# Two transformer blocks in fp32 on one core: earlier weight splits, norm scales left in PSUM, and a reworked program end

## The reference

```python
def hybrid_layer(x, ...):                       # first block
    h = rmsnorm(x, g_pre_mix);  proj = h @ w_in
    y_a = s5_mixer(...); y_b = short_conv_mixer(...); y_c = forgetting_attention(...)
    merged = sum(sigmoid(gate_i) * (y_i @ w_branch_i) for the 3 branches)
    x = x + rmsnorm(merged @ w_out, g_post_mix)
    ff = square(relu(rmsnorm(x, g_pre_mlp) @ w_ff1)) @ w_ff2
    return x + rmsnorm(ff, g_post_mlp)

def second_block(x, ...):
    h = rms_norm(x, norm_mix_pre);  z = h @ w_in
    # chunk_band_attention, hgrn2, spatial_gating, rg_lru_branch: 4 branches of width 256
    merged = sum(sigmoid(gate_n) * (out_n @ w_branch_n) for the 4 branches)
    x = x + rms_norm(merged @ w_out, norm_mix_post)
    gt, up = split(rms_norm(x, norm_ffn_pre) @ w1)
    return x + rms_norm((silu(gt) * up) @ w2, norm_ffn_post)
```

## Time and profile before

| | us |
|---|---|
| three runs | 3702.2, 3705.89, 3710.4 |
| median | 3705.89 |
| the profiled execution | 3706.02 |
| span in its profile | 3704.3 |
| mean PEclk | 0.977 |

### The profile page before, as it was taken

How to read it: one execution, slowest core, us unless ns; L and a number is a source line. 1 busy time by engine, 2 the same in 40 slices (tenths; PEclk the granted TensorE clock), 3 DMA queues, 4 the chain that set the end, 5 groups by cost and what they waited for, 6 DMA issues and landing times. The chain is left out here.

```text
span 3704.3 us, 40483 instructions
## 1 busy us (share of the span) xinstructions
PE 3508.4 (95%) x16092; PEld 2820.4 (76%) x16092; DVE 1446.7 (39%) x1591; ACT 873.6 (24%) x1068; POOL 895.3 (24%) x421
## 2 busy tenths in 40 slices
PE   6989999998998999999989998999999899999996
PEld 5767788887876888888867877777777588888885
DVE  7723565655315222212153446463552521121123
ACT  3112222223313111111232222212342411111111
POOL 2101111111341222222312114231245222222223
PEclk9979999999999999999999999999999999999998
DMA  2534343324421111111224213113253211111122
GB/s 109 148 70 158 109 147 126 100 88 167 146 91 73 47 45 51 45 51 45 91 97 124 92 66 120 63 69 125 99 199 136 74 45 51 45 51 45 45 79 102
DMA packets 105056, 336.81 MB, mean 91 GB/s; under 512 B 15232, under 2 KB 25344, under 8 KB 104848
## 3 DMA queue, kind: packets, MB, share of 16 engines
q1 hardware_dynamic: 101344, 329.78, 26.4%
q10 hardware_dynamic: 3584, 5.25, 0.5%
HBM read 250.37 MB, written 87.62 MB: 91 GB/s over the span
## 5 line engine op out<-in xcount | busy, mean ns | idle before, releaser
L270 POOL TENSOR_TENSOR w_lo<-w_raw,w_hi 128x1024 fp32r<-128x1024 f32 x276 | 686.6, 2488 | 2492.2 <-ACT w_hi L268 2492.2
L307 PE MATMUL pair<-act_hi,w_hi 128*128 128x512 f32 x2992 | 971.4, 406 | 18.9 <-issue 7.0
L307 PE MATMUL pair<-act_lo,w_hi 128*128 128x512 f32 x2992 | 946.5, 397 | 0.0
L307 PE MATMUL pair<-act_hi,w_lo 128*128 128x512 f32 x2992 | 945.1, 397 | 0.0
L307 PEld LDWEIGHTS pair<-act_lo,w_hi 128*128 128x128 f32 x2992 | 566.4, 189 | 138.6
L307 PEld LDWEIGHTS pair<-act_hi,w_lo 128*128 128x128 f32 x2992 | 565.4, 189 | 138.7
L307 PEld LDWEIGHTS pair<-act_hi,w_hi 128*128 128x128 f32 x2992 | 547.7, 190 | 142.7 <-issue 23.5
L268 ACT CAST w_hi<-w_raw 128x1024 fp32r<-128x1024 f32 x276 | 288.9, 1047 | 785.9 <-PE pair L307 709.6
L571 DVE TENSOR_TENSOR p<-pair,rs 128x1024 f32<-128x1024 f32 x100 | 122.1, 1221 | 435.6 <-PE pair L307 428.5
L1791 DVE TENSOR_TENSOR f2v<-pair,rs 128x1024 f32<-128x1024 f32 x42 | 51.4, 1224 | 346.6 <-PE pair L307 346.6
L307 PE MATMUL pair<-f1hh,w_hi 128*128 128x512 f32 x480 | 147.8, 389 | 0.0
(11 more groups left out here) (464 smaller groups left out, 4086.6 us busy)
## 6 DMA issues: line engine op xcount, KB each, us to landing
w_raw<-in_stream SPq DMA_DIRECT2D x278, 512.0 KB, 3.5
proj<-p SPq DMA_DIRECT2D x101, 512.0 KB, 2.6
m2g<-proj SPq DMA_DIRECT2D x32, 512.0 KB, 4.7
foxx<-proj SPq DMA_DIRECT2D x32, 256.0 KB, 5.5
m1g<-proj SPq DMA_DIRECT2D x16, 512.0 KB, 3.3
x<-f1y SPq DMA_DIRECT2D x16, 512.0 KB, 2.6
act_lo<-x SPq DMA_DIRECT2D x16, 512.0 KB, 7.8
m1l<-mixed SPq DMA_DIRECT2D x12, 512.0 KB, 9.2
```

The lines of the kernel that those rows point to most:

```text
L270: nc.gpsimd.tensor_tensor(wlo[:, slot, :], raw[:, slot, :], whi[:, slot, :].bitcast(F32), ALU.subtract).then_inc(s_split, 1)
L307: last = nc.tensor.matmul(out_pair[:, h * HALF:(h + 1) * HALF], wt, a[:, h * HALF:(h + 1) * HALF], start=k == 0 and n_pass == 0, stop=k == ...
```

## The change

Five edits.

1. `split_unit` of unit b+2 is issued at the last tile of unit b, which is the product that frees the slot, and ahead of that block's `evict`; the split of b+1 at the first tile of b goes. In `TwoBlocks` both blocks issue the split at their end, POOL's subtraction in four pieces of 256 columns.
2. The row of scales isn't copied to SBUF: DVE's multiplications in `bridge` read it in PSUM. `lag` for half 1 is 8 instead of 4, so that all tiles of the head's second block for half 1 come after the step loop.
3. `mix_out`'s tail evictions go from DVE (L1741) to ACT.
4. In the last bridge the gain is multiplied in with the scale (one `scalar_tensor_tensor` from PSUM), the residual is added in a second instruction, for k = 1, 3 and 5 on POOL, and every half of 256 KB is stored by itself. The last square goes into the sums by a matmul of its own instead of through POOL.
5. The stream's last two empty units aren't fetched, and the final waits are for two fewer.

```diff
     def split_unit(b, slot, fills, pieces=1):
...
+        n = KT * P // pieces
+        for at in range(0, KT * P, n):
+            last = nc.gpsimd.tensor_tensor(wlo[:, slot, at:at + n], raw[:, slot, at:at + n],
+                                           whi[:, slot, at:at + n].bitcast(F32), ALU.subtract)
+        last.then_inc(s_split, 1)
...
                 if w == 0:
-
-                    split_unit(b + 1, 1 - slot, i * (per_turn // 2) + ((base + n // 8 + 1) // 2 + 1))
                     fetch_unit(b + 3, 1 - slot)
...
+                if w == 7 or (not packed and k == tiles - 1):
+                    split_unit(b + 2, slot, i * (per_turn // 2) + ((base + n // 8 + 2) // 2 + 1))
                 yield
             evict(i, o, out_pair, ready, reads.mark)
...
             if not self.begun:
                 self.begun = True
-                split_unit(b + 1, 1 - slot, (b + 1) // 2 + 1)
-                fetch_unit(b + 3, 1 - slot)
+                if b == 0:
+                    split_unit(1, 1, 1)
+                if not self.final:
+                    fetch_unit(b + 3, 1 - slot)
...
-                    if o == 0:
-                        split_unit(b + 2, slot, b // 2 + 2)
+                    if not self.final:
+                        split_unit(b + 2, slot, b // 2 + 2, 4)
+                    if o == 0 and not self.final:
                         fetch_unit(b + 4, slot)
...
-        y_scale = [A.mark(A.after(spread).copy(r[:, halves[0]], bank[0][:])), None]
+        y_scale = [spread, None]
...
-        lag = (2, 4)
+        lag = (2, KT)
...
-            V.mark(V.after(y_scale[h]).tensor_tensor(yk, yk, r[:, half], ALU.mult))
+            if not next_gain:
+                scaled = V.mark(V.after(y_scale[h], x_ready[k]).scalar_tensor_tensor(yk, yk, col(gain, k), bank[h][:],
+                                                                                     ALU.mult, ALU.mult))
+                if k in (1, 3, 5):
+                    added[h, k] = G.mark(G.after(scaled, x_ready[k]).tensor_tensor(yk, yk, x(k)[:, half], ALU.add))
+                else:
+                    added[h, k] = V.mark(V.then().tensor_tensor(yk, yk, x(k)[:, half], ALU.add))
+                SP.wait_ge(*added[h, k])
+                stores[k % 2].mark(SP.dma_start(out_dram[k][:, half], yk))
+                return
+            V.mark(V.after(y_scale[h]).tensor_tensor(yk, yk, bank[h][:], ALU.mult))
...
-            if k == 3:
+            if k == 3 and next_gain:
                 sums = half_sums(bank[1][:], squares[:, halves[1]], True, True, summed)
+            if k == 2 and not next_gain:
+                half_sums(bank[1][:], squares[:, halves[1]], True, False, summed)
+                sums = half_sums(bank[1][:], last_square[0], False, True, last_square[1])
             if k == 4:
                 root = half_root(1, bank[1][:], 1.0 / D, sums)
             if k == 6:
-                spread = half_spread(1, bank[1][:], root)
-            if k == 7:
-                y_scale[1] = A.mark(A.after(spread).copy(r[:, halves[1]], bank[1][:]))
+                y_scale[1] = half_spread(1, bank[1][:], root)
...
-            square_sum(dst, sq[:, half], squares[:, half], read(V.after(ready).tensor_copy(dst, psum)))
+            square_sum(dst, sq[:, half], squares[:, half], read(A.after(ready).copy(dst, psum)))
...
+                if not next_gain and o and half.start:
+                    a = read(V.after(ready).tensor_tensor(dst, dst, psum, ALU.add))
+                    last_square.extend([sq[:, half], A.mark(A.after(a, G.last()).activation(sq[:, half], dst, ACT.Square))])
+                    return
...
-    for s, n in ((0, (used["units"] + 4) // 2), (1, (used["units"] + 3) // 2)):
+    for s, n in ((0, (used["units"] + 2) // 2), (1, (used["units"] + 1) // 2)):
         SP.wait_ge(s_raw[s], 16 * n)
```

More of the change, by code:

```diff
@@ L263, in _build, with split_unit @@
     used = {"units": 0, "blocks": 0}
-    def split_unit(b, slot, fills):
+    def split_unit(b, slot, fills, pieces=1):
         nc.scalar.wait_ge(s_raw[slot], 16 * fills)
@@ L269, in split_unit @@
         nc.gpsimd.wait_ge(s_whi, b + 3)
-        nc.gpsimd.tensor_tensor(wlo[:, slot, :], raw[:, slot, :], whi[:, slot, :].bitcast(F32),
-                                ALU.subtract).then_inc(s_split, 1)
+        n = KT * P // pieces
[3 more added lines that the diff above has]
+        last.then_inc(s_split, 1)
     def fetch_unit(b, slot):
@@ L391, in _build, with __init__ @@
     class TwoBlocks:
-        def __init__(self, tiles, rhs):
-            self.tiles, self.rhs = tiles, rhs
+        def __init__(self, tiles, rhs, final=False):
+            self.tiles, self.rhs, self.final = tiles, rhs, final
             self.base, self.begun = used["units"], False
@@ L463, in half_spread, with bridge @@
         return PE.mark(last)
-    def bridge(tail, tail_evict, y, squares, x, x_ready, r, sq, gain, out_dram, next_gain, head=None, head_evict=None):
+    def bridge(tail, tail_evict, y, squares, x, x_ready, sq, gain, out_dram, next_gain, head=None, head_evict=None,
+               last_square=None):
         halves = [slice(h * HALF, (h + 1) * HALF) for h in range(2)]
@@ L1714, in __init__ @@
             self.x = sb(at, name + "v", [P, 2, L])
-        def scale_row(self):
-            return self.x[:, 1, :]
         def square_row(self, h, n):
@@ L1740, in tail_evict @@
             dst = y[:, 6 + o, half]
-            square_sum(dst, sq[:, half], squares[:, half], read(V.after(ready).tensor_copy(dst, psum)))
+            square_sum(dst, sq[:, half], squares[:, half], read(A.after(ready).copy(dst, psum)))
         stage(3, 2, 2, KT, rhs, evict, per={A: 2, G: 2})
         bridge(TwoBlocks(KT, act_rhs), tail_evict, y, squares, lambda k: late.hl[:, k, :].bitcast(F32), x_ready,
-               late.scale_row(), late.square_row, gain, out_dram, next_gain, TwoBlocks(KT, act_rhs), head_evict)
+               late.square_row, gain, out_dram, next_gain, TwoBlocks(KT, act_rhs), head_evict)
     def first_hidden(late, gated):
@@ L1834, in mlp @@
                     e.wait_ge(s_mm, used["units"] + 2)
-        tail = TwoBlocks(tiles, hidden_rhs)
+        last_square = []
+        tail = TwoBlocks(tiles, hidden_rhs, final=not next_gain)
         bridge(tail, tail_evict, acc, squares, lambda k: act_lo[:, k, :].bitcast(F32), x_ready,
-               late.scale_row(), late.square_row, gain, out_dram, next_gain,
-               TwoBlocks(KT, act_rhs) if next_gain else None, head_evict)
+               late.square_row, gain, out_dram, next_gain,
+               TwoBlocks(KT, act_rhs) if next_gain else None, head_evict, last_square)
     def first_rows(dst, row, buf):
@@ L1991, in _stream @@
         parts += [w1[g:g + m], np.pad(w2[:, g:g + m], ((0, 0), (0, 8 - m), (0, 0), (0, 0)))]
-    tiles = np.concatenate([p.reshape(-1, P, P) for p in parts] + [np.zeros((3 * 8, P, P), np.float32)])
+    tiles = np.concatenate([p.reshape(-1, P, P) for p in parts] + [np.zeros((8, P, P), np.float32)])
     return _units(tiles)
```

## The result

The changed kernel takes 3719.87 us (median of five, 3718.85 to 3730.13), the one before 3705.51 (3702.2 to 3710.4). The ratio over all runs is 1.0048, 95% interval 1.0031 to 1.0065 (of the two medians alone 1.0039): slower. The forecast was 3712 with a range of 3688 to 3721, 47% for no change and 29% for slower. The time is inside the range, but the kernel became 14.4 us longer, where 6.1 were forecast. The profiled execution has a span of 3717.5 us, 13.2 more than before.

What follows compares the result with a forecast made beforehand. PE, busy 95% of the span, was taken to bound the kernel. Merge 2 +23.7, bridges -6.4, the end -9.5, the chain -1.7 and woven parts 0 gave +6.1 on 3706.02: 3712 us, range 3688 to 3721.

Steps and rivals of the forecast that it cites:

- Merge 2: Merge 2: POOL's moved subtraction stops DVE's two-SBUF-input addition seven times, +15.2 us; with slow clock +23.7.
- The clock: Merge 2: PE idle times of 2.96 us followed by half clock in five of seven cases, +8.5 us.
- Bridges: Bridges A, B, C: `w_lo` waits go, the scale copy is saved, lag 8 costs some; -6.4 us in all.
- The lag's price: Bridges A to C: with `lag` 8, four half tiles no longer fill PE's `act_lo` waits, +4.2 us.
- the sign that I named for it: Bridges: more of PE's idle time released by `act_lo` for half 1 would show the forecast right.
- The end: Last bridge to program end: no `w_lo` wait or slow stretch behind it, shorter additions and stores, -9.5 us.
- The chain: First block's step-size chain: the split now runs before L582, which POOL's subtraction had slowed, -1.7 us.
- the term for the woven parts: Attention, scans, merge 1, feed-forward: later ACT work and DVE meeting POOL are covered by PE's products; 0, +-4 us.
- slower elsewhere too: Scans and attention: subtractions at unit ends also stop DVE where PE waits for it, 2.2 us each; 3722, chance 20%.

Runs made afterwards that it cites:

- e1: The changed kernel with merge 2's last gated product written to PSUM instead of SBUF: 3696.05 us, 0.9969 of the kernel before.
- e13: e5b with the early split in merge 2 as well, whole subtractions: 3712.60 us, 1.0012 of the kernel before.
- e2: The changed kernel with the splits of all products behind the eviction again, the bridges' still early: 3702.84 us, 0.9985 of the kernel before.
- e8b: e5b with the lag for half 1 back at 4 instead of 8: 3683.95 us, 0.9940 of the kernel before.
- e14: e5b with early splits in the woven products too, late in both merges: 3694.38 us, 0.9961 of the kernel before.
- e5b: The changed kernel with early splits only in looped stages and bridges, late in woven products and merges: 3689.10 us, 0.9950 of the kernel before.
- e15: e14 with one split, at unit 39's end in the second block, put behind its eviction: 3693.68 us, 0.9957 of the kernel before.
- e3: The changed kernel with POOL's subtraction cut from 1024 columns to 32: 3635.43 us, 0.9809 of the kernel before.
- e4: The kernel before with POOL's subtraction cut from 1024 columns to 32: 3628.86 us, 0.9792 of the kernel before.
- e10: The changed kernel with POOL's subtraction in quarter pieces in every unit: 3682.15 us, 0.9938 of the kernel before.
- e9: The same program as e5b, measured a second time: 3687.33 us, 0.9949 of the kernel before.
- e7b: The kernel before with POOL's subtraction in four pieces of 256 columns in every unit: 3681.27 us, 0.9928 of the kernel before.
- e12: e5b with lag 4 and POOL's subtraction in eight pieces of 128 columns in every unit: 3654.61 us, 0.9865 of the kernel before.

## Why the prediction was right and wrong

- **Merge 2, right in mechanism and size.** Chain, lead (0.12 us measured, 0.08 forecast), length of the addition (3.36 against 3.40) and PE's idle time (2.92 against 2.96) came as worked out, seven times; e1 and e13 show cause and price, 24 us each.
- **The clock, right in sum by luck.** 24.9 - 14.9 = 10.0 us against 8.5, five of seven followed by slow stretches, as chosen. But the reason given, that 2.96 lies on the low side of 2.40 and 2.82, isn't one: the same 2.92 did both, and two of the five slow stretches were twice as long as reckoned.
- **Bridges, right in sign, too small** (-9.7 against -6.4). `w_lo` went as forecast. e2 keeps the quarter pieces, the reads from PSUM and the lag, and its bridges are 0.7 us longer than before, where the forecast had -0.6 for these; so the early split ahead of the bridges gave some 10.4 us, where I had put 5.8 for the waits alone. The lag's price was right in size (3.8 to 8.3 by e8b, against 4.2). The idle time released by `act_lo` hardly moved as a whole (31.3 to 30.5 us), so the sign that I named for it didn't show.
- **The end, right**: -10.7 against -9.5; by e2, 6.4 of it is the early split (5.1 forecast) and 4.3 the other edits (4.4 forecast). From the last product's end to the spread 8.7 us passed instead of the forecast 9.1.
- **The chain, right in sign**: -3.9 against -1.7; two stops went (L582, L587), and slow clock with them. With whole subtractions it comes only with early woven splits (-3.8 in e14, -0.1 in e5b).
- **The step that failed** is the term for the woven parts: "PE has a unit's 11 us of products before it needs most of them. I take 0, with +-4." The woven stretches came to about +12.5 us; the misses of the other terms took 5.5 of that back (merge 2 +1.2, bridges -3.3, the end -1.2, the chain -2.2), so that the sum was only 7.1 us off. Two premises were wrong. The first is a reading: "most CASTs of weights already start at the end of the product that frees their slot". It was 110 of 276, and the change made it 249. The second is the price, one CAST or 1.05 us later. That held for the copy (+0.96), but a CAST also makes what stands behind it wait for PE: the squares stood behind 4.96 us of waiting and then the CAST. The cover isn't there where a stage's own chain runs through the three engines and PE waits for that chain, not for a product's eviction. Moving a split ahead of `evict` also moves it ahead of whatever the stage has put into ACT's and POOL's queues before the next tile.
- **What the runs put in its place**: a CAST ahead of other work in ACT's queue (2.15 us at the squares, shown by e15, and 0.96 at a copy), POOL's queue held ahead of a scan's additions (1.4 us; e3, e4 and e10 speak for it, no run moved that one split), and slow stretches behind them. The rival "slower elsewhere too" named the place, and 3722 was near; but it named DVE's stops as the cause. At the three places looked at PE waited for what stood in the queues of ACT and POOL behind a split, and in the feed-forwards 107 us of stops cost nothing. I gave it 20%.
- **Only part of the +12.5 us hangs on the woven splits.** The second block's +8.6 does: with these splits early that stretch grew by 8.6, 5.1 and 2.8 us (the change, e14, e1) with +4.9 to +5.6 of idle time each, with them late by -0.7 to +0.9 (e2, e5b, e9, e13) with none. The +3.2 of the other stretches doesn't: they are 3.2 and 3.1 us longer in e5b and e9 too, where the woven splits are late, and 2.3 us shorter in e13. What makes them is open, and so is how much of the +8.6 is chance in the clock, as three programs with the same queue order there gave 2.8 to 8.6.

## What to carry to other kernels

An instruction that waits for the bottleneck engine should not stand in a shared queue ahead of work that the bottleneck itself will wait for: list, stage by stage, what is queued behind it, also in the stages that the edit was not meant for. Before moving an instruction of POOL, look for DVE instructions with two SBUF inputs within its length, and for chains that they belong to; splitting it in four shortened the stop from 2.1 to 0.5 us, and putting one operand in PSUM took it away. To price contention, cut the suspected work and time the kernel: here 79 us hung on POOL's subtractions, and the list of waits names them for 9.2. Don't take the price from the length of the stops: those in the feed-forwards cost nothing, those in merge 2 their whole length and slow stretches besides.

## What the runs showed of the hardware

- POOL's subtractions, 276 of 2.4 us, cost the kernel before 79 of 3706 us (e4) although POOL is busy 24% of the time. Beside one, DVE instructions with two SBUF inputs of 0.3 to 1.2 us take up to 2.2 us more (L799 2.43 instead of 0.29 us, L635 3.45), 102 us in all; the waits for `w_lo` and for POOL's queue are in the 79 too.
- Thirty such stops of 2.1 us in the first feed-forward made the stretch 0.0 us longer.
- A DVE instruction with one of its inputs in PSUM, started 0.13 us behind the same subtraction, wasn't slowed at all (1.22 us, e1).
- A quarter of one POOL instruction takes 0.74 us instead of 0.60 (e7b), an eighth 0.46 instead of 0.30 (e12).
- Seven idle times of PE of 2.92 us in the same loop were followed by full clock twice and half clock five times, for 3.4 or 6.8 us, and in e13 in the same order.
